# A macaron encoder layer in fp32 on one core: six direct tile pairs per feed-forward become four, and the direct phase of ScalarE and VectorE is written in another order

## What is computed

```python
def _swiglu(h, w_up, w_down):
    gate, up = jnp.split(h @ w_up, 2, axis=-1)
    return (jax.nn.silu(gate) * up) @ w_down

x = x + 0.5 * _swiglu(_rms(x, g_ffn1[l]), w_up1[l], w_down1[l])
# ... mixer: window attention, Fourier mixing, gates, w_out ...
x = x + 0.5 * _swiglu(_rms(x, g_ffn2[l]), w_up2[l], w_down2[l])
return _rms(x, g_final)
```

## Time and profile before

| | |
|---|---|
| median of 3 runs | 988.84 us (988.77 to 990.72) |
| the profiled execution | 989.13 us, of which its span is 987.3 us |
| PE busy | 977.3 us (99% of the span) |
| DVE busy | 680.8 us (69%) |
| ACT busy | 446.2 us (45%) |
| POOL busy | 184.5 us (19%) |
| granted PE clock | 0.999 of full speed, mean |

### The profile page before, as it was taken

How to read it: one execution, slowest core, us unless ns; L and a number is a source line. 1 busy time by engine, 2 the same in 40 slices (tenths; PEclk the granted TensorE clock), 3 DMA queues, 4 the chain that set the end, 5 groups by cost and what they waited for, 6 DMA issues and landing times.

```text
span 987.3 us, 16127 instructions
## 1 busy us (share of the span) xinstructions
PE 977.3 (99%) x5780; PEld 870.5 (88%) x5780; DVE 680.8 (69%) x935; ACT 446.2 (45%) x679; POOL 184.5 (19%) x108
## 2 busy tenths in 40 slices
PE   8999999999999999999999999999999999999997
PEld 7889999999888888888888888888999999988887
DVE  5897989999534346678884564479798989943322
ACT  6534444446323235458773343443354444642322
POOL 1332434340011010000000002242333434000101
PEclk9999999999999999999999999999999999999999
DMA  7513424223433364122123343331333332333222
GB/s 223 164 43 95 118 85 127 85 85 92 133 89 94 110 168 121 53 86 64 43 75 96 106 127 102 94 105 51 97 110 104 108 91 79 106 118 100 84 61 86
DMA packets 188711, 98.26 MB, mean 100 GB/s; under 512 B 13368, under 2 KB 186472, under 8 KB 188672
## 3 DMA queue, kind: packets, MB, share of 16 engines
q1 hardware_dynamic: 186736, 94.40, 32.9%
q10 hardware_dynamic: 1872, 3.32, 0.9%
q0 software_dynamic: 64, 0.03, 0.0%
HBM read 95.61 MB, written 2.11 MB: 99 GB/s over the span
## 4 chain that ended last, share of the span: by engine, by line
PE 98%; DMA 1%; issue 1%; POOL 0%; ACT 0%; POOLq 0%; ACTq 0%; DVE 0%
PE bank L1582 19%; PE bank L1583 19%; PE bank L1592 19%; PE bank L1686 11%; PE bank L1682 11%; PE bank L1680 11%; PE bank L1901 1%; PE bank L1802 1%; PE bank L1803 1%; PE bank L1807 1%; DMA onehot<-in_onehot_dram 1%; PE bank L1587 1%; PE bank L1889 0%; PE bank L1888 0%; PE bank L1919 0%
## 5 line engine op out<-in xcount | busy, mean ns | idle before, releaser
L614 ACT ACTIVATE w_hi<-raw 128x1024 fp32r<-128x1024 f32 (+2 forms) x202 | 181.5, 902 | 233.1 <-PE bank L1592 147.6
L1039 DVE TENSOR_TENSOR w_lo<-raw,w_hi 128x1024 fp32r<-128x1024 f32 (+2 forms) x138 | 147.8, 1074 | 138.2 <-ACT w_hi L614 136.6
L1682 PE MATMUL bank<-t_lo,w_hi 128*128 128x256 f32 x896 | 224.7, 283 | 0.0
L1680 PE MATMUL bank<-t_hi,w_hi 128*128 128x256 f32 x896 | 224.6, 283 | 0.0
L1682 PEld LDWEIGHTS bank<-t_lo,w_hi 128*128 128x128 f32 x896 | 172.0, 192 | 0.2
L1680 PEld LDWEIGHTS bank<-t_hi,w_hi 128*128 128x128 f32 x896 | 172.0, 192 | 0.2
L1686 PE MATMUL bank<-t_hi,w_lo 128*128 128x256 f32 x896 | 144.0, 283 | 0.0
L1582 PE MATMUL bank<-a_hi,w_hi 128*128 128x512 f32 (+1 forms) x374 | 140.1, 379 | 0.0
L1583 PE MATMUL bank<-a_lo,w_hi 128*128 128x512 f32 (+1 forms) x374 | 139.4, 377 | 0.0
L1531 POOL TENSOR_TENSOR ssum<-ssum,sq 128x512 f32<-128x512 f32 x20 | 30.6, 1530 | 498.9 <-ACT sq L651 498.9
L1686 PEld LDWEIGHTS bank<-t_hi,w_lo 128*128 128x128 f32 x896 | 123.6, 192 | 0.0
(11 more groups left out here) (246 smaller groups left out, 1478.8 us busy)
## 6 DMA issues: line engine op xcount, KB each, us to landing
raw<-in_w_down_dram SPq DMA_DIRECT2D x48, 384.0 KB, 3.0
raw_b<-in_w_up_dram SPq DMA_DIRECT2D x64, 256.0 KB, 3.6
raw<-in_w_up_dram SPq DMA_DIRECT2D x64, 256.0 KB, 3.5
raw<-in_w_up_dram SPq DMA_DIRECT2D x24, 512.0 KB, 3.8
raw<-in_w_in_dram SPq DMA_DIRECT2D x22, 512.0 KB, 3.7
raw<-in_w_down_dram SPq DMA_DIRECT2D x32, 128.0 KB, 2.2
raw<-in_w_out_dram SPq DMA_DIRECT2D x8, 512.0 KB, 3.4
x_rows<-in_x_dram SPq DMA_DIRECT2D x4, 512.0 KB, 7.0
```

Of the source, the lines that this page charges most:

```text
L614: return nc.scalar.activation(dst, src, ACT.Copy, scale=scale)
L1039: vec.tensor_tensor(w_lo[:, s, 0:nk, :], raw[:, s, 0:nk, :], w_hi[:, s, 0:nk, :].bitcast(F32), ALU.subtract).then_inc(w_lo_ready, 1)
L1680: nc.tensor.matmul(out_ap, w_hi[:, slot, at_ + k, :], hi[:, k, :], start=first and k == 0, stop=False, skip_group_check=not first)
L1682: nc.tensor.matmul(out_ap, w_hi[:, slot, at_ + k, :], lo_[:, k, :], start=False, stop=False, skip_group_check=not first)
```

## The change

`DIRECT` goes from 6 to 4 and with it `PAIRS` from 16 to 18, in both FFNs. So granules 8 to 11 disappear and two frames are added behind. `direct_pairs` of ACT and DVE loses its steps for granules 8 to 11, for pairs 4 and 5, and gets another order for the rest. Constants that follow from `DIRECT` (semaphore counts, loop counts, which buffer slot a group has) change with it.

```diff
-DIRECT = 6
+DIRECT = 4
 PAIRS = FK - DIRECT
@@ ScalarE, direct_pairs
                 direct_hi(r, 7)
+                t_rounded(r, T_B11)
                 if r == 0:
                     act.wait_ge(row_ready, 1)
                     act.dma_start(bias_rows, bias_row[:, :]).then_inc(bias_stored, 16)
-                t_rounded(r, T_B11)
-                direct_hi(r, 8)
                 t_rounded(r, T_1)
                 t_rounded(r, T_B21)
-                direct_hi(r, 9)
+                silu(r, 2)
                 t_rounded(r, T_2)
-                silu(r, 2)
                 t_rounded(r, T_4)
-                direct_hi(r, 10)
                 t_rounded(r, T_3)
                 t_rounded(r, T_B22)
+                group_hi(r, 0, G0)
                 silu(r, 3)
-                direct_hi(r, 11)
-                group_hi(r, 0, G0)
-                silu(r, 4)
                 group_hi(r, 0, G1)
                 group_hi(r, 0, G2)
-                silu(r, 5)
@@ VectorE, direct_pairs
                 gate(r, 1)
-                swish(r, 0)
-                direct_lo(r, 6)
-                up(r, 1)
                 for i in range(HK):
                     normed_h(nrm, i)
-                swish(r, 1)
-                direct_lo(r, 7)
+                swish(r, 0)
+                up(r, 1)
                 for i in range(HK, DK):
                     normed_h(nrm, i)
-                direct_lo(r, 8)
+                direct_lo(r, 6)
+                t_rest(r, T_B11)
+                swish(r, 1)
                 gate(r, 2)
+                direct_lo(r, 7)
+                t_rest(r, T_2)
+                t_rest(r, T_B21)
                 up(r, 2)
+                sums(r, 0)
                 swish(r, 2)
-                t_rest(r, T_B11)
-                t_rest(r, T_2)
-                direct_lo(r, 9)
-                gate(r, 3)
-                t_rest(r, T_B21)
-                up(r, 3)
-                direct_lo(r, 10)
-                swish(r, 3)
                 t_rest(r, T_4)
                 t_rest(r, T_1)
-                direct_lo(r, 11)
-                sums(r, 0)
-                gate(r, 4)
+                gate(r, 3)
+                group_lo(r, 0, G0)
                 t_rest(r, T_3)
-                group_lo(r, 0, G0)
-                up(r, 4)
-                swish(r, 4)
+                group_lo(r, 0, G1)
                 t_rest(r, T_B22)
-                group_lo(r, 0, G1)
-                gate(r, 5)
+                up(r, 3)
                 group_lo(r, 0, G2)
                 sums(r, 1)
-                up(r, 5)
-                swish(r, 5)
+                swish(r, 3)
```

## The result

The change makes the kernel slower: 1000.32 us (999.95 to 1000.5, four runs) against 988.89 (988.77 to 990.72, four runs), a ratio of 1.0109 with an interval of 1.0096 to 1.0121. The predicted 1001.0 is 0.7 too high. The profiled execution took 1000.36 us with a span of 998.5, so the span grew by 11.2 us over the earlier trace rows. PE now has 3.2 us less to do and loses 14.4 us more to waits and slow work.

The account below looks back on a forecast made before the run. PE was taken to bound the kernel, busy 99% of the span. Waits of 5.0, 2.2 and 0.5 us make 7.7 per FFN, 15.4 - 3.2 = +12.2: 989.13 to 1001.3, median 988.84 to 1001.0; range 995.0 to 1003.5.

Parts of the forecast that it names:

- PE's saving: Both FFNs: swapping a direct pair for frame work saves PE 0.80 us, four swaps 3.2 us.
- DVE's queue with POOL's turns: First frame of each FFN: DVE's work plus POOL's turns makes G0's low part 5.0 us late for PE.
- the walk: DVE's list from 29.30 to G0's low part: 22.4 us of work plus 10.6 of POOL's turns, ready at 62.3.
- lower end: Direct phase: if POOL lost a turn at each close call, PE's waits would be 6.6 us per FFN, time 998.8.
- cross-check: G0's low part reckoned from its readiness in the kernel before: 69.9 - 11.4 + 3.7 = 62.2.
- The wait for `u2`, 2.2 us: First frame: DVE has `u2` done at 70.7, PE needs it at 68.5 and waits 2.2 us.
- The clock: Rival, chance 0.09: PE's clock falls in the first frame's wait, up to 4.0 us per FFN, 1001 to 1009.
- main case: DVE's queue late with POOL's turns in both FFNs: 7.7 us each, 998.8 to 1001.5, predicted 1001.0; chance 0.71.
- `z_read`, 0.5 us: First frame's seventh product: PE waits 0.5 us for DVE's `z_read`, behind the second frame's G0, G3 and G1 splits.
- DVE without idle between 30 and 70: Direct phase of the first FFN: DVE has no idle time between 30 and 70; idle there would show wrong.
- The turns cost: Rival, chance 0.13: POOL's turns take 6.9 us of DVE as before, G0 ready at 58.6, time 993.4.
- Nothing is late: Rival, chance 0.07: POOL's T sums hide in DVE's reads of PSUM, no lateness at 57.26, time 985.6.

Follow-up runs that it names:

- the fill by POOL: Changed kernel, but POOL fills T_1, T_2, T_4 and T_3 with a constant by memset in place of subtracting; 986.32 us, ratio 0.997.
- six pairs of cover: Kernel before with its six direct pairs, but ACT's and DVE's lists in the changed kernel's new order; 988.9 us, ratio 1.0007.
- the kernel with the filled wait: Changed kernel with 14 matmuls of 512 columns into an unused bank in PE's wait for G0's low part; 1000.22 us, ratio 1.0113.
- with the old order: Four direct pairs, but ACT and DVE keep the order of the kernel before, without the steps of the removed granules and pairs; 1001.23 us, ratio 1.0124.
- the kernel with the order of need: Changed kernel with DVE's weight splits, `sums`, G0 and G1 early, `swish`, T_3 and B22 late, T sums on POOL; 998.54 us, ratio 1.0099.

## Why the prediction was right, and where it was not

**PE's saving** (0.80 us per swapped pair, 3.2 in all) is right to 0.4 us. With the T sums filled in, 2.8 of it show in the span, and twelve frames of the changed kernel still take 10.08 us each.

**DVE's queue with POOL's turns** is the right cause. The fill by POOL takes the lateness away and leaves everything else, six pairs of cover take it away too, and four pairs are late in either order. Its size was 5.0 us and measured 4.2 (0.65 and 3.5). Put beside the walk, the turns cost as follows, each a DVE duration less the same one undisturbed:

| turn | forecast | measured | from |
|---|---|---|---|
| T_1 | 1.8 | 1.6 | 4.29 less 2.73 |
| T_2 | 2.34 | 1.6 | 2.81 less 1.21 |
| T_4 | 2.34 | 2.3 | idle ahead of 48.30 |
| T_3 | 1.8 | 2.2 | 3.42 less 1.21 |
| S2 and S4 | 2.34 | 2.2 | 1.78 less 0.68; 3.42 less 2.35 |
| sum | 10.6 | 9.8 | |

The rows for the last three turns (DVE):

```profile
48.30 3.42 DVE L1037 TENSOR_TENSOR t_lo<-t_sum,t_hi 128x1024 fp32r<-128x1024 f32 x1 [2.28 <-POOL t_sum L1528]
...
54.58 1.78 DVE L1117 TENSOR_TENSOR a_t<-ga_t,ua_t 128x512 f32<-128x512 f32 x1
56.28 3.42 DVE L1037 TENSOR_TENSOR t_lo<-t_sum,t_hi 128x1024 fp32r<-128x1024 f32 x2
```

With the copy of the norm factor 0.16 earlier (29.14), 29.14 + 22.4 + 9.8 is the 61.4 that the trace has, within 0.1. The four T sums are 7.7 of the 9.8. The fill freed 7.0, because with it DVE idles 0.59 us for ACT's rounding of T_2, an idle time that POOL's turns had hidden. The term that was over-sized is T_2's turn. The walk gave POOL its turn at the end of the instruction that was running, and it got it two instructions later, where `gate` hid 0.6 of it. The prediction had this as its lower end, "if it lost one like this at each close call". Ahead of G0 it lost one here, not at each; a second one was lost behind G0, at the second frame's S2.

The prediction's cross-check (62.2) could not have caught this. Its 3.7 is the walk's own 10.6 less the 6.9 of the old order, so it tests the 22.4 us of work and not the turns.

The Trainium skill (SBUF — State Buffer, section "SBUF: two separate sides") would have given POOL the turn at 40.87, since whoever starts first holds the ports for the whole instruction. This trace does not agree for T_2, as it did not at 38.16 in the kernel before; it does for S2 at 54.13, where `swish` stood at once. The same section of the Trainium skill has a DVE instruction outside the two-port modes contend only if it has two SBUF inputs, and only against a GpSimd one that reads SBUF. On this the traces agree: `gate` at 42.60, which reads PSUM, took its 0.68 beside POOL, and the splits at 38.24 and 39.37 took their 1.21 beside POOL's fills.

**The wait for `u2`, 2.2 us**, is the step that failed. The walk put POOL's turn for the second frame's S2 ahead of `swish` 3 and `u2`. The rows of POOL and DVE say otherwise:

```profile
67.26 2.28 POOL L1535 TENSOR_TENSOR raw<-raw 128x512 f32<-128x512 f32 x1 [9.77 <-DVE raw L1181]
...
67.71 0.67 DVE L1117 TENSOR_TENSOR a_t<-gb_t,ub_t 128x512 f32<-128x512 f32 x1
68.31 0.41 DVE L1198 TENSOR_TENSOR u_t<-bank,p_t 128x256 f32<-128x256 f32 x1
```

POOL asked at 67.26, `swish` 3 went ahead of it, and `u2`, which reads PSUM, ran beside it. So `u2` was done at 68.7, not at 70.7: about 0.9 of this because G0 was earlier, about 1.2 because the turn did not stand in its way. Without that turn the forecast's own 2.2 are 1.0, and this is what the kernel with the filled wait has from start to start (0.8 by the row at 68.77). In the changed kernel there is no wait, since PE came later by the fallen clock.

**The clock** had 0.09 as a rival and fell in both FFNs. The prediction looked at the row where the clock was half within 3 us of PE's last work, and gave too small a chance to a fall in a wait of that length: it came in both FFNs here (3.32 and 3.33 us of waiting) and in both with the old order (5.1 us). What saved the number is the rest of the rival's own sentence, that slower products hide in the waits behind them. It allowed up to 4.0 us per FFN; the filled wait shows 0.1 us in the whole run, inside the spread. So the main case's total, 7.7 per FFN, came out as 7.1 with another composition. That DVE's list sets the time is what the prediction had right; which of PE's idle or slow stretches fills it is second. That the two totals are as close as 0.6 is in part luck: 0.9 too much for G0 and 1.2 too much at `u2` stand against 0.7 for the second frame's G0, for which the forecast had no term, 0.3 at `z_read`, and 0.1 of slow start behind each of five waits (the last section).

**`z_read`, 0.5 us**, measured 0.8 from start to start with the filled wait and 0.3 without. **The second FFN** repeats the first to 0.01 us in the long wait (3.32 and 3.33). **Later frames** don't wait, so DVE catches up, as forecast. **DVE without idle between 30 and 70** was wrong, and idle time there was one of the prediction's own signs of being wrong: DVE idled 2.28 us at 48.30, for POOL's T_4, and 1.95 us up to 70.67, for ACT and so for POOL's S2. Neither refutes the cause, since both waits are for POOL's sums. The walk put T_4 down as a turn that holds up `swish` 1; it was a wait of `t_rest` of T_2, which happened to be as long. The waits list does not look as forecast either: four new waits, 4.0 us per FFN and none for `u2`, in place of 7 to 8.

**The other rivals** fell. The turns cost 9.8, not 6.9. "Nothing is late" is what the fill by POOL shows: 986.3 measured for a case forecast at 985.6, so the price was nearly right and the condition was not met.

## What to carry to other kernels

Before cover is taken from a bound engine, sum the whole list of the engine that works under it, and add the turns that a third engine takes from it; a busy share of 69% said nothing about it. Moving the third engine's work onto the late one can shorten the late one's list, if a turn costs more than doing the work, but here most of the gain came only together with an order in which things are finished as they are needed. When the bound engine's clock falls in a wait, look first at who releases it next: where that was the same late engine, keeping the clock up was worth nothing; where little waiting was left, the fall cost 1.0 us.

## What the runs showed that I had not expected

- POOL can lose several turns in a row, and when it does is open. Asked at 39.89, its T_2 let two DVE instructions pass; in the kernel with the order of need T_1 asked at 36.31, during `swish`, and two splits of 1.14 us passed before it ran. S2 of the first frame, asked at 54.13, got the very next turn; S2 of the second, asked at 67.26, like the first 0.15 us into the second `sums` instruction, let `swish` pass. What decides it was not tried. T_1 in the kernel with the order of need (timeline of POOL), with the instruction that let it in and stood for it (timeline of DVE, 4.88 us in place of 2.73):

```profile
36.31 5.05 POOL L1535 TENSOR_TENSOR t_sum<-t_sum 128x1024 f32<-128x1024 f32 x1 [12.55 <-DVE t_sum L1173]
```

```profile
39.02 4.88 DVE L1173 SCALAR_TENSOR_TENSOR t_sum<-xT,consts,rstd 128x512 f32<-128x512 f32 x4
```

- A fill by POOL costs DVE nothing (38.24 and 39.37, 1.21 us each beside it), a subtraction of the same size costs 1.6 to 2.2 us where a DVE instruction stands for it.
- The half clock lasted 5.5 us and more of dense work after a wait of 3.3 us, and 3.5 us (61.79 to 65.3) after the wait of 5.08 in the old order. The same waits filled with matmuls that nobody reads kept it at 1.00. A wait of 2.39 us left the clock up in the first FFN of the kernel with the T sums on VectorE, and in the second it fell 1.4 us after PE was at work again (0.51 from 682 to 685). The kernel with the order of need and the sums on POOL did the same around its wait of 2.84 us (1.00 in the first FFN, 0.52 from 685 to 688 in the second). So the length of the wait alone did not tell.
- After each wait looked at PE also starts slowly: the second matmul follows 0.22 us behind the first (68.77 to 68.99), the others 0.12. The busy time of PE counts the slow matmuls as work: 981.0 us with 3.2 us less to do.
